# Selected-key attention in a fused transformer kernel: pairs of heads on two row halves, mask by matmul, unnormalised probabilities, fewer input tiles

## The reference

```python
proj = x @ w_in           # columns [q 1024 | k 128 | v 128 | q_idx 512 | k_idx 64 | w_idx 8]
dots   = einsum('bthd,bsd->bths', q_idx, k_idx)              # 8 index heads of width 64
scores = einsum('bths,bth->bts', relu(dots), w_idx)          # causal, NEG_BIG elsewhere
_, sel = lax.top_k(scores, 64)
logits = einsum('btkgd,btskd->btkgs', q, k[sel]) * 64 ** -0.5 # 16 heads, 2 key-value heads
probs  = softmax(where(valid, logits + rel_bias[bucket(t - s)], NEG_BIG))
out    = einsum('btkgs,btskd->btkgd', probs, v[sel]) @ w_out
```

## Time and profile before

| what | us |
|---|---|
| median of 3 runs | 1776.7 |
| lowest and highest | 1774.08, 1779.76 |
| the profiled execution, its own time | 1769.84 |
| its span | 1768.0 |
| TensorE busy in the span | 1688.8 (96%) |
| VectorE, ScalarE, GpSimd busy | 1155.5, 892.7, 44.7 |
| mean granted TensorE clock | 0.971 |

### The profile page before, as it was taken

How to read it: one execution, slowest core, us unless ns; L and a number is a source line. 1 busy time by engine, 2 the same in 40 slices (tenths; PEclk the granted TensorE clock), 3 DMA queues, 4 the chain that set the end, 5 groups by cost and what they waited for, 6 DMA issues and landing times.

```text
span 1768.0 us, 32661 instructions
## 1 busy us (share of the span) xinstructions
PE 1688.8 (96%) x12119; PEld 1552.0 (88%) x12119; DVE 1155.5 (65%) x1962; ACT 892.7 (50%) x1436; POOL 44.7 (3%) x103
## 2 busy tenths in 40 slices
PE   7999999998899998999999989999899998989998
PEld 7898999896689997999879889998799998689997
DVE  4868877758577777655566865555665557565555
ACT  7456555543565556444466454444644445364443
POOL 4000000002100000000000000000000000000000
PEclk9999999987999999999999999999899999799999
DMA  9446666643256666766655547666466665136662
GB/s 247 143 127 205 192 183 189 166 120 95 72 155 179 189 189 194 214 188 178 190 189 152 188 127 211 182 181 186 120 184 188 187 178 148 54 106 195 188 188 73
DMA packets 390508, 293.53 MB, mean 166 GB/s; under 512 B 22987, under 2 KB 362340, under 8 KB 390048
## 3 DMA queue, kind: packets, MB, share of 16 engines
q1 hardware_dynamic: 386912, 280.57, 54.3%
q0 software_dynamic: 2816, 10.24, 1.7%
q10 hardware_dynamic: 704, 1.67, 0.3%
HBM read 291.38 MB, written 1.07 MB: 165 GB/s over the span
## 4 chain that ended last, share of the span: by engine, by line
PE 70%; DVE 6%; ACT 2%; issue 1%; POOL 0%; DVEq 0%; ACTq 0%
PE ps L376 22%; PE ps L377 21%; PE ps L378 21%; DVE w_lo L367 1%; PE ps L432 1%; PE ps L1208 1%; DVE H L535 1%; PE ps L1742 1%; PE ps L1741 1%; ACT L512 0%; DVE SQ L528 0%; ACT SQ L507 0%; DVE A L1389 0%; PE ps L1227 0%; PE ps L1471 0%
## 5 line engine op out<-in xcount | busy, mean ns | idle before, releaser
L376 PE MATMUL ps<-x_hi,w_hi 128*128 128x256 f32 x2672 | 762.8, 285 | 6.2 <-DVE x_lo L1924 2.4
L377 PE MATMUL ps<-x_hi,w_lo 128*128 128x256 f32 x2672 | 759.6, 284 | 0.0
L378 PE MATMUL ps<-x_lo,w_hi 128*128 128x256 f32 x2672 | 759.5, 284 | 0.0
L367 DVE TENSOR_TENSOR w_lo<-raw,w_hi 128x1024 fp32r<-128x1024 f32 x534 | 648.9, 1218 | 34.7 <-ACT w_hi L360 34.2
L360 ACT ACTIVATE w_hi<-raw 128x1024 fp32r<-128x1024 f32 x534 | 544.1, 1047 | 97.7 <-PE ps L378 87.6
L376 PEld LDWEIGHTS ps<-x_hi,w_hi 128*128 128x128 f32 x2672 | 516.6, 193 | 13.4 <-issue 5.9
L377 PEld LDWEIGHTS ps<-x_hi,w_lo 128*128 128x128 f32 x2672 | 516.3, 193 | 4.4
L378 PEld LDWEIGHTS ps<-x_lo,w_hi 128*128 128x128 f32 x2672 | 516.0, 193 | 0.0
L645 ACT ACTIVATE sl<-gs 128x256 f32<-128x256 f32 x88 | 36.9, 420 | 398.2 <-DVE gs L749 398.2
L749 DVE TENSOR_TENSOR gs<-ps,R 128x256 f32<-128x256 f32 x88 | 37.4, 425 | 276.8 <-PE ps L378 276.8
L376 PE MATMUL ps<-w_hi,h_hi 128*128 128x512 f32 x528 | 207.1, 392 | 1.3 <-DVE h_lo L673 1.3
(11 more groups left out here) (254 smaller groups left out, 1361.7 us busy)
## 6 DMA issues: line engine op xcount, KB each, us to landing
raw<-in_ffn_w_up SPq DMA_DIRECT2D x176, 512.0 KB, 3.8
raw<-in_ffn_w_down SPq DMA_DIRECT2D x132, 512.0 KB, 4.5
raw<-in_ffn_w_gate SPq DMA_DIRECT2D x88, 512.0 KB, 4.6
raw<-in_hgrn_w_in SPq DMA_DIRECT2D x32, 512.0 KB, 4.7
raw<-in_gmlp_w_in SPq DMA_DIRECT2D x32, 512.0 KB, 4.3
raw<-in_gmlp_w_out SPq DMA_DIRECT2D x16, 512.0 KB, 3.8
raw<-in_dsa_w_in SPq DMA_DIRECT2D x13, 512.0 KB, 4.2
raw<-in_hgrn_w_out SPq DMA_DIRECT2D x8, 512.0 KB, 3.6
```

The source lines that it names most:

```text
L367: nc.vector.tensor_tensor(w_lo[:, s, :], raw[:, s, :], w_hi[:, s, :].bitcast(F32), ALU.subtract)\
L376: pe.matmul(o, whi, xhi, start=first, stop=False, skip_group_check=not group)
L377: pe.matmul(o, wlo, xhi, start=False, stop=False, skip_group_check=not group)
L378: return pe.matmul(o, whi, xlo, start=False, stop=last, skip_group_check=not group)
```

## The change

- The input chunks of the stage go from 17 to 15. The index key (64 columns) and the index weights (8 columns) share one chunk, the keys of the two key-value heads another; values are computed as a feature tile and transposed. Output feature tile `j` now holds head `j` in rows 0 to 63 and head `j + 8` in rows 64 to 127, so query chunks and output-weight chunks are fetched as two half chunks each.
- The index key is copied to rows 64 to 127 by a matmul with the identity. Dots and logits are issued for two heads in turn, one on each half of the array's rows.
- ScalarE reads 13 of the 15 feature tiles from PSUM without scaling, VectorE two; the norm factor of the query goes into later scales. The dots stand between the feature tiles, and the eight selection rounds beside tiles 6 to 13.
- The mask is added by one matmul per head (identity times mask, fp32r, 384 columns) into the PSUM of the logits. GpSimd's additions go; VectorE subtracts the position bias, read backwards, in the pass that scales.
- Exponentials are no longer summed or divided. The values have a column of ones behind each head's 64 columns; the output has tokens on its rows, its 65th column is the sum, VectorE divides by it, and TensorE transposes the result.
- One loop with the pairs in it replaces the calls of the shared attention functions. The output projection of a pair is issued in two parts of six matmuls. The output banks are finished `BY_ROWS`, and the next stage's first transposes wait for three of the four additions instead of two.
- The latent attention's semaphores are renamed and count on from the new stage's totals.

```diff
-    phase("dsa", [twice(ds_in, D), twice(ds_in, D + 64), twice(ds_in, 1792)]
-          + [feat(ds_in, 1280 + j * P) for j in range(4)] + [feat(ds_in, 1152), feat(ds_in, 1856, 8)]
-          + [feat(ds_in, j * P) for j in range(8)] + [rows(T["dsa_w_out"][0], k) for k in range(8)])
+    phase("dsa", [feat(ds_in, 1792, 72)] + [feat(ds_in, 1280 + j * P) for j in range(4)]
+          + [feat(ds_in, D), feat(ds_in, 1152)] + [two(ds_in, j * 64, (j + 8) * 64) for j in range(8)]
+          + [[(lambda s: s[0:64], ds_out[j * 64:j * 64 + 64, :]), (lambda s: s[64:P], ds_out[(j + 8) * 64:(j + 8) * 64 + 64, :])]
+             for j in range(8)])
...
-        ORDER = {n: BY_HALF if n in ("hgrn", "ffn0", "dsa") else BY_ROWS for n in ENDS}
+        ORDER = {n: BY_HALF if n in ("hgrn", "ffn0") else BY_ROWS for n in ENDS}
...
-                    pe.wait_ge(*rows_of(n, 4 if q > 1 else 2 if n in ("ffn0", "ds", "ffn1") else 3))
+                    pe.wait_ge(*rows_of(n, 4 if q > 1 else 2 if n in ("ffn0", "ds") else 3))
...
+            tile_(0)
+            tile_(1)
+            pe_spread(pe, "ds")
+            tile_(2)
+            tile_(3)
+            ds_read(pe, 0)
+            pe.matmul(ps[64:P, 4, 0:L], c_ident[0:64, 0:64], kIw[0:64, :], start=True, stop=True, tile_position=(0, 64))\
+                .then_inc(S("ds_shift"), 1)
...
+            tile_(4)
+            dots(0)
+            dots(1)
+            tile_(5)
+            dots(2)
+            dots(3)
+            tile_(6)
...
+            def logits(j):
...
+                for i in range(2):
+                    pe.matmul(ps[:, i, 0:ATT_W], ident_r, mask_r, start=True, stop=False)
+                for a, b, c in ((0, 0, P), (P, P, L)):
+                    for i in range(2):
+                        r = slice(64 * i, 64 * i + 64)
+                        mm = pe.matmul(ps[:, i, a:a + c], qA[r, j, b:b + P], kA[r, 0:c], start=False, stop=a > 0)
...
+            def values(j, i):
+                pe.wait_ge(S("at_pt"), 2 * j + i + 1)
+                if j and not i:
+                    pe.wait_ge(S("at_xlo"), j)
...
+                o = lambda tb: ps[:, 3, (2 * tb + i) * 65:(2 * tb + i) * 65 + 65]
+                p = lambda m: pTA[:, i, m * P:m * P + P]
+                pe.matmul(o(0), p(0), vA[:, 0, i, :], start=True, stop=True)
+                pe.matmul(o(1), p(1), vA[:, 0, i, :], start=True, stop=False)
+                mm = pe.matmul(o(1), p(2), vA[:, 1, i, :], start=False, stop=True)
...
+            for i in range(11):
+                if i < 8:
+                    logits(i)
+                if 0 <= i - 2 < 8:
+                    turn(i - 2)
+                if 0 <= i - 1 < 8:
+                    probs(i - 1, 0)
+                if 0 <= i - 3:
+                    project(i - 3, 0)
+                if 0 <= i - 1 < 8:
+                    values(i - 1, 0)
+                    probs(i - 1, 1)
+                if 0 <= i - 3:
+                    project(i - 3, 1)
+                if 0 <= i - 1 < 8:
+                    values(i - 1, 1)
...
+                l = lgA[:, j % 2, :]
+                parts = (l[:, 0:2 * P].rearrange("p (i w) -> p i w", i=2), l[:, 2 * P:].rearrange("p (i w) -> p i w", i=2))
+                for tb, (a, w, bias) in enumerate(((0, P, toe[:, j:j + 9:8, P - 1::-1]), (P, L, toe[:, j:j + 9:8, ::-1]))):
+                    nc.vector.scalar_tensor_tensor(parts[tb], ps[:, 0:2, a:a + w], sc[:, tb:tb + 1], bias, ALU.mult, ALU.subtract)\
+                        .then_inc(S("at_lsb"), 1)
+                for tb in range(TB):
+                    dve.wait_ge(S("at_lsb"), 2 * j + tb + 1)
+                    nc.vector.tensor_reduce(mnA[:, j % 2, tb, :], parts[tb], axis=AX_X, op=ALU.min).then_inc(S("at_mn"), 1)
...
+            for i in range(10):
+                if i < 8:
+                    bounds(i)
+                if 0 <= i - 2 < 8:
+                    dve.wait_ge(S("at_xhi"), i - 1)
+                    nc.vector.tensor_tensor(x_lo[:, i - 2, :], ps[:, 3, 0:L], x_hi[:, i - 2, :].bitcast(F32), ALU.subtract)\
+                        .then_inc(S("at_xlo"), 1)
+                if i >= 2:
+                    split_lo(dve, c0 + 16 + i)
+                if 0 <= i - 1 < 8:
+                    weigh_out(i - 1)
...
-        def dsa_pool(pool):
-            pool.wait_ge(S("ds_mask"), 1)
-            pool.wait_ge(S("in_toe"), 16)
-            for h in range(NH_A):
-                if h >= 2:
-                    pool.wait_ge(S("da_lsb"), h - 1)
-                nc.gpsimd.tensor_tensor(comb[:, h % 2, 0:P], toe[:, h, P - 1::-1], maskA[:, 0:P], ALU.add)
-                nc.gpsimd.tensor_tensor(comb[:, h % 2, P:ATT_W], toe[:, h, ::-1], maskA[:, P:ATT_W], ALU.add)\
-                    .then_inc(S("ds_comb"), 1)
```

More of the change, by code:

```diff
@@ L110, in twice, with two @@
     def twice(w, a):
+        return two(w, a, a)
+    def two(w, a, b):
         v = lambda s, o: s.rearrange("p (k m) -> p k m", k=KT)[:, :, o:o + 64]
-        return [(lambda s: v(s, 0), w[:, :, a:a + 64]), (lambda s: v(s, 64), w[:, :, a:a + 64])]
+        return [(lambda s: v(s, 0), w[:, :, a:a + 64]), (lambda s: v(s, 64), w[:, :, b:b + 64])]
     def rows(w, r, a=0):
@@ L1326, in dsa_pe, with dots @@
-            pe.wait_ge(S("ds_q"), 8)
-            pe.wait_ge(S("ds_rl"), 8)
-            def logits(h, o):
-                q = slice(64 * (h % 2), 64 * (h % 2) + 64)
-                k = kA[q, h // 8, :]
-                pe.matmul(o[:, 0:P], qA[q, h // 2, 0:P], k[:, 0:P], start=True, stop=True)
-                return pe.matmul(o[:, P:ATT_W], qA[q, h // 2, P:L], k, start=True, stop=True)
-            att_pe(pe, "da", NH_A, 2, c0 + 17, logits, lambda h, tb: vA[:, tb, 64 * (h // 8):64 * (h // 8) + 64])
+            def dots(j):
+                for i in range(2):
+                    h = 2 * j + i
+                    if h < 2:
+                        pe.wait_ge(S("ds_ku"), 1)
+                        pe.wait_ge(S("ds_w"), 1)
+                    elif h < 4:
+                        pe.wait_ge(*once("r_done", "ds"))
+                    else:
+                        pe.wait_ge(S("ds_rl"), h - 3)
+                ds_read(pe, 1 + j)
+                for a, b, c in ((0, 0, P), (P, P, L)):
+                    for i in range(2):
+                        h = 2 * j + i
+                        r = slice(64 * i, 64 * i + 64)
+                        mm = pe.matmul(ps[:, 4 + h % 4, a:a + c], qI[r, j, b:b + P], (kIw, kIu)[i][r, 0:c], start=True, stop=True)
+                mm.then_inc(S("ds_dot"), 1)
@@ new lines, in dsa_pe @@
+            dots(0)
[4 more added lines that the diff above has]
+            tile_(6)
+            tile_(7)
+            tile_(8)
+            ds_read(pe, 6)
+            pe.wait_ge(S("ds_rl"), 8)
+            for tb in range(TB):
+                mm = pe.transpose(ps[:, 4, tb * P:tb * P + P], vF[:, tb * P:tb * P + P], c_ident)
+            mm.then_inc(S("ds_vps"), 1)
+            for t in range(9, DS_TILES):
+                tile_(t)
+            def logits(j):
+                if j == 0:
+                    ds_read(pe, 13)
+                    ds_read(pe, 5)
+                    pe.wait_ge(S("ds_mask"), 1)
+                    pe.wait_ge(S("ident_r"), 1)
+                else:
+                    pe.wait_ge(S("at_lsb"), 2 * j)
+                ds_read(pe, 7 + j)
+                for i in range(2):
+                    pe.matmul(ps[:, i, 0:ATT_W], ident_r, mask_r, start=True, stop=False)
+                for a, b, c in ((0, 0, P), (P, P, L)):
+                    for i in range(2):
+                        r = slice(64 * i, 64 * i + 64)
+                        mm = pe.matmul(ps[:, i, a:a + c], qA[r, j, b:b + P], kA[r, 0:c], start=False, stop=a > 0)
+                mm.then_inc(S("at_lps"), 1)
@@ new lines, in probs @@
+            def probs(j, i):
+                pe.wait_ge(S("at_exp"), 4 * j + 2 * i + 2)
+                if j or i:
+                    pe.wait_ge(S("at_pt"), 2 * j + i)
+                else:
+                    ds_read(pe, 14)
+                p = prA[:, j % 2, :]
+                for m, at in enumerate((i * P, 2 * P + i * L, 2 * P + i * L + P)):
+                    mm = pe.transpose(ps[:, 2, m * P:m * P + P], p[:, at:at + P], c_ident)
+                mm.then_inc(S("at_tps"), 1)
+            def values(j, i):
+                pe.wait_ge(S("at_pt"), 2 * j + i + 1)
+                if j and not i:
+                    pe.wait_ge(S("at_xlo"), j)
+                if not j and not i:
+                    pe.wait_ge(S("ds_v"), 2)
+                    ds_read(pe, 11)
+                o = lambda tb: ps[:, 3, (2 * tb + i) * 65:(2 * tb + i) * 65 + 65]
[3 more added lines that the diff above has]
+                mm = pe.matmul(o(1), p(2), vA[:, 1, i, :], start=False, stop=True)
+                if i:
+                    mm.then_inc(S("at_ops"), 1)
@@ new lines, in turn, with project @@
+            def turn(j):
+                pe.wait_ge(S("da_on"), j + 1)
+                for tb in range(TB):
```

(18 more changed lines are left out.)

238 lines of the change are left out of this document (139 added, 99 removed).

## The result

| | before | changed |
|---|---|---|
| median of 4 runs each | 1776.52 us | 1749.44 us |
| lowest to highest | 1774.08 to 1779.76 | 1747.81 to 1754.17 |
| profiled execution | 1769.84 us | 1747.85 us |
| stage, first transposes to the next stage's | 146.3 us | 123.7 us |

The ratio is 0.9866 (95% interval 0.9839 to 0.9893): 1.3% faster, where 1755.5 us and 1.2% were forecast. A repeat on another chip gave 0.9873 (0.9849 to 0.9898).

What follows compares the result with a forecast made beforehand. TensorE, busy 96%, gains only from waits, low clock or needless work; VectorE's rounds bind before the mask. 18.1 + 3.3 - 0.2 = 21.2 us off 1769.84 gives 1748.6, or 1755.5 us on the median's footing; range 1742 to 1768.

Steps and rivals of the forecast that it cites:

- What bounds the stage: Selected-key stage: TensorE's 5.50 us idle ends when VectorE has the mask; VectorE's selection rounds bind after the dots.
- Fewer tiles, up to the mask: First feature tile to mask: about 50.3 us for 68.5, 18.1 us won, bounds 15 to 20.
- The reads moved to ScalarE: Eight query-tile reads of about 0.4 us hide on ScalarE, taking 0.34 us from each VectorE round's period.
- Short pieces: Query chunks loaded as two DMAs of 256-byte pieces: taken as zero delay, range 0 to 4.7 us.
- Row halves overlap: Logits of a pair take 0.85 us, 1.70 if serial; rival without overlap or with slow bias: 1762 us, chance 0.13.
- Values 0.68 a head: Attention values: three full-array fp32 matmuls per head take 0.68 us, range 0.35 to 1.0.
- VectorE not slower on a reversed bias: Two bias passes about 1.1 us, two reductions 1.0; rival of slow bias or no overlap: 1762 us, chance 0.13.
- Period 7.2: Attention at full clock: one pair of heads takes 7.2 us against 7.99, with 6.6 us of TensorE work.
- Clock: half from the first logits, back inside turn 3: Start of attention: half clock for 20 to 30 us; turn 3 takes 10.3 us if the clock returns inside it.
- Rival that the clock stays down: Attention: the clock stays at half until the stage ends, 31 us later than forecast, 1786.5 us; chance 0.07.
- Attention 72.3, 3.3 won: All attention turns sum to 72.3 us against 75.56, 3.3 us won.
- end 0.2 lost: Stage end: finishing output by row block, with transposes waiting for a third addition, loses 0.2 us (0 to 0.7).

Runs made afterwards that it cites:

- e7_reads_on_dve: Changed kernel with the eight query tiles read from PSUM by VectorE again, one behind each selection round: 1754.1 us, ratio 0.9904, stage 127.3 us.
- e8_two_chains: Changed kernel with the index sums of the two query halves each waiting only for their own predecessor on VectorE: 1752.86 us, stage 122.4 us.
- e6_long_packets: Changed kernel with query and output-weight chunks each fetched in one unbroken DMA, heads paired wrongly: 1748.04 us, stage 123.6 us.
- e5_no_mask_mm: Changed kernel without the two mask matmuls per pair, so attention is unmasked: 1745.8 us, stage 120.2 us, period 6.63 us.
- e1_xlo_first: Changed kernel with VectorE making the low half of the turned output before the row minima: 1751.11 us, ratio 0.989, stage 118.9 us.
- e3_fill: Changed kernel with 29 extra, unread matmuls ahead of TensorE's waits in the attention's first three turns: 1741.56 us, ratio 0.9833, stage 117.2 us.
- e2_by_half: Changed kernel with output finished by column half again and the next transposes waiting for two additions: 1751.1 us, stage 124.3 us.
- e4_head_major: Changed kernel with a pair's query-key matmuls issued head by head instead of interleaved: 1749.07 us, stage 124.8 us, period 7.05 us.

## Why the prediction was right, by its own steps

- **What bounds the stage.** Right that it is VectorE: `e7_reads_on_dve` put eight reads (2.7 us) back on it and got 2.66 later logits, `e8_two_chains` took 0.56 off. Wrong in one reading: the 5.50 us in before did not end "when VectorE has the mask" but with the last read of a query tile, 0.8 us before the mask was done. The sum is not touched, since it went from logits to logits: it took the reads out and put the mask's 0.94 in front of the new first logits.
- **Fewer tiles, up to the mask: 50.3 us, 18.1 won.** Measured 51.03 us from first tile to first logits (before 68.5), 17.4 won. Shift and transposes took 0.77 (0.9 forecast), four heads' dots 1.51 (1.6), rounds 2.84 (2.83). Most of the miss is in the weighing, 0.95 us a head for 0.83: four heads make 0.5 us of it. The other 0.2 is the step from the finished mask to the first matmul (401.79 to 402.01), which the sum left out; together they are why TensorE waits 2.4 and not 1.6. The 14 operations in 5.78 us of the earlier trace rows held a pause of 0.09 between one head's sums and the next; the changed kernel's is 0.20. `e8_two_chains` shows that waiting for both sums makes the pause; why it is longer than in before, where both were waited for too, no run shows.
- **The reads moved to ScalarE: hidden.** Right, between the tiles TensorE has no wait.
- **Short pieces: zero of 0 to 4.7.** Right, by `e6_long_packets`. The Trainium skill ("DMA: Bandwidth & Descriptors", Specifications) puts the smallest transfer at line rate at 512 B. No run here shows a cost of going below it at the 130 to 166 GB/s that this stage asks for; whether it would bind at full rate was not tried.
- **Row halves overlap: 0.85 for the logits of two heads.** 0.86. The mask matmuls took 0.52 a pair for 0.34; `e5_no_mask_mm` gives 0.40 back.
- **Values 0.68 a head (0.35 to 1.0).** 0.69 for the first head (442.58 to 443.27), 0.22 a matmul; 0.59 for the second. With 65 moving columns a matmul takes as long as the earlier trace rows with 128: the narrower moving side bought nothing. So the values did not come near the prediction's lower bound of 0.35.
- **VectorE not slower on a reversed bias.** 1.14 for two passes (1.1 forecast), minima 1.00 (1.0). From the end of the logits to the end of the low half 2.5 us, to the values 2.65, for 2.8 with hops.
- **Period 7.2.** 7.03, with TensorE work of 6.5 (6.6 forecast) and a wait of 0.50 (0.65), its cause as forecast; `e1_xlo_first` shows the cause. Inside the work single terms missed and partly cancelled: mask and logits 1.38 for 1.2, each half of the projection 1.47 for 1.37, three probability transposes 0.26 (443.27 to 443.53) for the 0.48 taken from the earlier trace rows.
- **Clock: half from the first logits, back inside turn 3.** Right, but for a fall 2.5 us later in this execution, and `e3_fill` shows it as the cause of 6.5 us. It came back 2.3 us after the first projection and not 5, so turn 3 took 8.96 for 10.3. Turns 0 to 2 took 20.55 for 20.4, and that is in part luck: the clock fell only 2.5 us after the first logits. In the repeat, at half clock from the first logits as forecast, they took 21.7. Turns 4 to the end 40.7 (431.52 to 472.2) for 41.6.
- **Rival that the clock stays down (0.07).** It did not; 0.55 to 428.40, then 1.00 to the end, though eight transposes stand in each turn. By the rule of the Trainium skill ("TensorE: Matmul & The Clock Gate", Part 4) that transpose mode does not count as busy, this case had something for it; the trace shows the clock at 1.00 over 43.80 us with these transposes in them, TensorE being busy for 40.33.
- **Attention 72.3, 3.3 won; end 0.2 lost.** 70.2 us to the last projection's end. The 75.56 of before run to the next stage's transposes (493.83); on that footing it is 70.43 (402.01 to 472.44), 5.1 won with the end's loss in it. Of the 2.1 us between 72.3 and 70.2, turn 3 makes 1.3 and the turns behind it 0.9. The end lost 0.32, by `e2_by_half`.

Sum: 17.4 + 5.1 = 22.5, forecast 21.2, with a miss of 0.7 up to the mask against one of 2.0 the other way behind it. That explains 1.3 of the 6.1 us between 1755.5 and 1749.4. The rest is footing. I put the sum on the median; the profiled execution of before was 6.7 us under its median, that of after 1.6 under. What made those other executions longer no trace shows. On the repeat the medians differ by 23.7, nearer to the stage's 22.5, so that the 27.1 of the first comparison holds some chance.

## What to carry to other kernels

Where a small engine-bound stretch leaves TensorE with holes, ask first what its clock does there: 8.4 us of matmuls that compute nothing shortened this stage by 6.5, and leaving out 42 narrow matmuls shortened the one before the change by 7.0. When a value that frees a bank and a value needed later are made on the same engine, make the first one first (0.75 us a turn here, at no cost). And when edits of 5 us sit in a kernel whose other stages vary by 3 to 5, measure the stage's own length in the trace beside the total.

## What the runs showed of the hardware

- Order does not matter for the overlap of the two row halves: four matmuls of one head, then four of the other, took the same 0.86 us as interleaved (`e4_head_major`, one execution).
- An fp32 matmul with 65 moving columns and a full stationary side took 0.22 us, as one with 128.
- The granted clock fell 2.5 us after the first logits in the changed kernel, behind a wait of 2.37 us; with an idle time of 5.04 (`e7_reads_on_dve`) the first logits were already at half clock (0.98 us for the two mask matmuls, against 0.59). In the repeat the same 0.98 stood behind a wait of 2.39, so the moment varies by some microseconds for one and the same program, and the stage with it (123.7 and 124.6). Over the eight traces with a wait of 1.8 to 2.4 us it lay between 0.4 us before and 3.1 us after the first logits.
- Untouched stages keep one of two lengths, by how long the clock stays at half (20.5 or 27.3 us in the latent attention, which is then 102.8 or 105.8 us long, in all fourteen traces); which of the two it was changed with edits elsewhere in the kernel.
